# Two transformer blocks on one core: the last block's down projection with tokens on partitions, its two last RMS scales as columns, and the output sent tile by tile

## The chip, the cores and the metric

The kernel runs on one NeuronCore of a Trainium2 chip. TensorE multiplies, VectorE (DVE), ScalarE (ACT) and GpSimd (POOL) work on tiles in SBUF and PSUM, SyncE (SP) only issues DMAs here. The metric is the device time of one execution in microseconds, as the median of several runs.

## What is computed

`x` is 512 tokens by 1024 features. It goes through two layers of a first block, a final RMS norm, and one layer of a second block. Only the end of the second block is touched:

```python
h = rmsnorm_2(x, norm_mlp_pre[l])
f = jnp.square(jax.nn.relu(h @ w_ff_in[l])) @ w_ff_out[l]      # 1024 -> 4096 -> 1024
x = x + rmsnorm_2(f, norm_mlp_post[l])                         # the output
```

## The kernel before, in words

Everything is float32, and nearly every product is three TensorE instructions in fp32r: each operand is split into a rounded part (`_hi`) and the rest (`_lo`), and `triple` (L345 to L347) adds hi·hi, hi·lo and lo·hi into one PSUM bank. A matmul has a stationary operand (128x128, loaded into the array) and a moving one (128 rows of 512 columns, streamed through). The profile names the moving operand first: `psG<-hid_hi,w_hi` streams `hid_hi` past weights from `w_hi`, `psG<-w_hi,h_hi` streams weights past activations.

Activations are kept as `xT`, with features on partitions and the 512 tokens along the free axis. `pe_feature`, `pe_part` and `pe_branch` stream activations and give features on partitions; `pe_token` streams weights and gives tokens on partitions.

Weights come in units of 1 MB. For each, SP issues two 512 KB DMAs into `raw` (`w_src`, L332), ACT rounds `raw` to `w_hi` (`split_hi`, L338) and POOL subtracts to `w_lo` (L2490). There are two buffers of each, so unit k+2 is split once TensorE is through with unit k: `split_next(act, k)` stands in ACT's program where that wait is to be made. TensorE spends 48 matmuls on a unit. `tick` counts its half units, `psum_free` gives back the two pairs of `psG` banks.

Buffers are laid out by hand: first `xT`, `h_hi`, `h_lo`, `raw`, `w_hi`, `w_lo`, then small tiles (`ident`, `ones`, ..., `par` with the norm gains as columns, ...), then an "arena" of 107 KB in which every stage puts its own tiles (`at(name, kb, ...)`, at whole or half kilobytes from its start). `h_hi` begins at byte 32896 of a partition, a multiple of 64, and so do `h_lo`, `raw`, `w_hi` and `w_lo`. The arena begins at byte 119200, which is 32 past a multiple of 64, and so every tile in it begins 32 past one.

The last MLP is done in two halves of 2048 hidden features: 8 units of `w_ff_in` (each in a `Fori` loop), whose result, relu'd and squared, is split into `hid2_hi` and `hid2_lo` at the arena's start, then 8 units of `w_ff_out`. A down unit is 8 blocks of hidden features by 256 output features. The hidden tiles are the moving operand, so `psG` holds output features on partitions, two banks at a time. DVE scales each bank by the squared inverse RMS of the pre norm (a row of 512 tokens repeated on all partitions, `rms`), keeps half 0 in `y2` and adds half 1.

What follows the last matmul (all after the half-1 loop in `second_pe`, `second_act`, `second_dve`): the squares of `y2` are folded together, summed over partitions with a matmul of ones (`sum_pe`, L448), ACT takes the root (L453), DVE the reciprocal of 128x512 (L457), `post_dve` scales and adds to `xT` (L2467, L2471), TensorE transposes `xT` back in 32 pieces (L2061), DVE copies to `x_out` (L2460), and four DMAs of 512 KB send it out (L1847).

Of the kernel before, what the change touches and what calls it, by code (L numbers as in the profile page):

```python
# [23 lines left out]
ds = bass.ds  # L24
# [84 lines left out]
def build_in(nc, io, ctx):  # L109
# [137 lines left out]
    y2 = at("y2", 64, [P, KD, S])  # L247
    r2 = at("r2", 80, [P, 2, S])
    hq2 = at("hq2", 84, [P, 2, S])
    x_out = at("x_out", 0, [P, TB, D])  # L250
# [584 lines left out]
    def setup_sync(sp):  # L835
        sp.dma_start(x_tok[:, :, :], io["x"].rearrange("a (t p) d -> p (a t) d", p=P)).then_inc(ld_x.sem, 16)
        rows = [(R_ATTN, io["attn_norm"].rearrange("l (k p) -> (l k) p", p=P)),
                (R_FFN, io["ffn_norm"].rearrange("l (k p) -> (l k) p", p=P)),
                (R_DA, io["da_norm"].rearrange("l (k p) -> (l k) p", p=P)),
                (R_HG, io["hg_norm"].rearrange("l (k p) -> (l k) p", p=P)),  # L840
                (R_LB, io["hg_lb_logits"].rearrange("d l (k p) -> (d l k) p", p=P)),
                (R_FINAL, io["final_norm"].rearrange("(k p) -> k p", p=P)),
                (R_PRE2, io["norm_mix_pre_2"].rearrange("l (k p) -> (l k) p", p=P)),
                (R_POST2, io["norm_mix_post_2"].rearrange("l (k p) -> (l k) p", p=P)),
                (R_MPRE2, io["norm_mlp_pre_2"].rearrange("l (k p) -> (l k) p", p=P)),
                (R_MPOST2, io["norm_mlp_post_2"].rearrange("l (k p) -> (l k) p", p=P))]
# [1037 lines left out]
    def second_pe(pe):  # L1884
# [149 lines left out]
        for half, vf, kf, vd, kd in ((0, V_FA, K_FA, V_DA, K_DA), (1, V_FB, K_FB, V_DB, K_DB)):  # L2034
            with pe.Fori(0, 4) as i:
                for s in range(2):
                    jm, b = step(JB + kf // 2, kf % 2, s)
                    pe_feature(pe, i + (UB + vf // 2), s, i + jm, b, h_hi, h_lo,
                               mlp_tile if half == 0 and s == 0 else None)
            if half == 0:  # L2040
                sum_pe(pe, DEPTH, 3, sq_x2)
            for c in range(4):
                jm, b = jn(kd + c)
                bank_ready(pe, jm, b)
                for v in range(2):
                    m, s = un(vd + 2 * c + v)

                    def hidden_tile(k, v=v, half=half):
                        pe.wait_ge(f2_lod.sem, HT2 * half + KD * v + k + 1)

                    pe_part(pe, m, s, b, hid2_hi, hid2_lo, KD * v, KD, v == 0, v == 1,
                            hidden_tile if c == 0 else None)
        sum_pe(pe, DEPTH, 4, sq)

        for h in range(2):
            for k in range(4):
                pe.wait_ge(x2_ok.sem, KD + 4 * h + k + 1)
                for t in range(TB):
                    if h and k == 0:
                        pe.wait_ge(o_cp.sem, t + 1)  # L2060
                    mm = pe.transpose(psH[:, t, k * P:(k + 1) * P], xT[:, 4 * h + k, t * P:(t + 1) * P],  # L2061
                                      ident[:, :])
                    if k == 3:
                        mm.then_inc(o_tr.sem, 1)
# [53 lines left out]
    def second_act(act):  # L2118
# [103 lines left out]
        for half, vf, kf in ((0, V_FA, K_FA), (1, V_FB, K_FB)):  # L2222
            with act.Fori(0, 4) as i:
                for s in range(2):
# [9 lines left out]
                    for j in range(2):  # L2234
# [4 lines left out]
            if half == 0:  # L2239
                rms_act(act, DEPTH, 3)  # L2240
            for k in range(8):
                if half and k % 2 == 0 and k:
                    act.wait_ge(y_ok.sem, k // 2 + 4)
                    square_pair(act, DEPTH, 3, k // 2 - 1, y2, sq)
                split_next(act, (V_DA, V_DB)[half] + k)
        act.wait_ge(y_ok.sem, 8)
        square_pair(act, DEPTH, 3, 3, y2, sq)
        rms_act(act, DEPTH, 4)
# [38 lines left out]
    def second_dve(dve):  # L2287
# [136 lines left out]
        for half, vf, kf, vd, kd in ((0, V_FA, K_FA, V_DA, K_DA), (1, V_FB, K_FB, V_DB, K_DB)):  # L2424
# [17 lines left out]
            for c in range(4):
                b = jn(kd + c)[1]
                if half and c >= 2:
                    fold(dve, DEPTH, 3, c - 1, sq)
                for j in range(2):
                    dve.wait_ge(tick.sem, Tn(vd + 2 * c + 1, j))
                    y = y2[:, 2 * c + j, :] if half == 0 else xtmp[:, j, :]
                    mm = tt(y, psG[:, 2 * b + j, :], rms[:, :], ALU.mult)
                mm.then_inc(psum_free[b].sem, 1)  # L2450
                if half:
                    dve.drain()
                    tt(y2[:, 2 * c:2 * c + 2, :], y2[:, 2 * c:2 * c + 2, :], xtmp[:, :, :], ALU.add)\
                        .then_inc(y_ok.sem, 1)
                    dve.drain()
        fold(dve, DEPTH, 3, 3, sq)
        post_dve(dve, 4, R_MPOST2)
        for n in range(8):
            dve.wait_ge(o_tr.sem, n + 1)
            dve.tensor_copy(x_out[:, n % TB, (n // TB) * S:(n // TB + 1) * S], psH[:, n % 4, :]).then_inc(o_cp.sem, 1)  # L2460
# [86 lines left out]
```

## Time and profile before

| | |
|---|---|
| median of 3 runs | 2508.78 us (2506.7 to 2508.93) |
| the profiled execution | 2509.79 us, its span 2507.60 us |
| TensorE busy | 2397.1 us, 96% of the span |
| DVE, ACT, POOL busy | 1298.4, 814.1, 862.1 us |
| mean granted TensorE clock | 0.978 |
| last matmul of the last product starts | 2471.32 us |

The span runs from the first to the last instruction of the execution; the device time is some 2 us more. Busy times overlap, so they do not add up to the span.

### The profile page before, as it was taken

What the parts mean: (1) busy time and instruction counts of PE and PEld (TensorE: products, weight loads), DVE (VectorE), ACT (ScalarE), POOL (GpSimd) and SP (SyncE); (2) the same over time, 40 slices, a digit from 0 to 9 for tenths busy, and PEclk for the clock granted to TensorE, in tenths of its full rate; (3) what the DMA queues carried; (4) which work ended last, traced back from release to release, by engine and by line L of the source; (5) the groups of instructions that cost most, each with busy time, mean ns of one, the idle gap of its engine ahead of it and who ended that gap; (6) DMA issues with size and microseconds to landing.
All of it is one profiled execution on the core that took longest, in us unless ns stands there. A gap on an engine that the chain in (4) does not pass through costs nothing.

```text
span 2507.6 us, 28122 instructions
## 1 busy us (share of the span) xinstructions
PE 2397.1 (96%) x11057; PEld 1911.8 (76%) x11057; DVE 1298.4 (52%) x1593; ACT 814.1 (32%) x909; POOL 862.1 (34%) x198
## 2 busy tenths in 40 slices
PE   6998999999998999989999999999999996999996
PEld 5888776788886888886667888887887774888884
DVE  6476344454446554664435534486457546631624
ACT  4232334332222332323343322222326523322320
POOL 2322122344443343222224444444323222443440
PEclk9999999999999999999999999999999997999997
DMA  5332133344445443322223444454844232444440
GB/s 123 85 77 58 34 68 68 84 91 93 100 100 118 126 99 87 68 51 47 62 61 85 100 100 94 90 139 114 172 101 82 63 74 52 96 89 101 94 91 34
DMA packets 200167, 217.50 MB, mean 87 GB/s; under 512 B 14456, under 2 KB 181512, under 8 KB 199304
## 3 DMA queue, kind: packets, MB, share of 16 engines
q1 hardware_dynamic: 200072, 216.16, 39.8%
q8 instruction: 69, 1.13, 0.2%
q14 instruction: 26, 0.21, 0.0%
HBM read 206.40 MB, written 9.73 MB: 86 GB/s over the span
## 4 chain that ended last, share of the span: by engine, by line
issue 57%; PE 26%; POOL 13%; DVE 3%; DVEq 1%; ACT 1%; POOLq 0%; ACTq 0%
POOL w_lo L2490 12%; PE psG L345 8%; PE psG L346 8%; PE psG L347 8%; PE psH L2004 1%; PE psH L1989 1%; DVE xT L2471 0%; DVEq L2469 0%; PE psH L2017 0%; PE psH L1957 0%; DVE rms L457 0%; DVE y L2467 0%; PE psH L448 0%; DVE sq L422 0%; POOLq L2487 0%
## 5 line engine op out<-in xcount | busy, mean ns | idle before, releaser
L2490 POOL TENSOR_TENSOR w_lo<-raw,w_hi 128x2048 fp32r<-128x2048 f32 x186 | 860.5, 4627 | 1592.9 <-ACT w_hi L338 1592.9
L345 PE MATMUL psG<-h_hi,w_hi 128*128 128x512 f32 x1640 | 653.8, 399 | 16.4 <-DVE h_lo L466 12.3
L338 ACT CAST w_hi<-raw 128x2048 fp32r<-128x2048 f32 x186 | 354.7, 1907 | 921.5 <-PE psG L347 907.1
L347 PE MATMUL psG<-h_hi,w_lo 128*128 128x512 f32 x1640 | 644.0, 393 | 0.0
L346 PE MATMUL psG<-h_lo,w_hi 128*128 128x512 f32 x1640 | 643.8, 393 | 0.0
L345 PEld LDWEIGHTS psG<-h_hi,w_hi 128*128 128x128 f32 x1640 | 310.6, 189 | 120.9 <-issue 45.3
L347 PEld LDWEIGHTS psG<-h_hi,w_lo 128*128 128x128 f32 x1640 | 310.9, 190 | 66.3
L346 PEld LDWEIGHTS psG<-h_lo,w_hi 128*128 128x128 f32 x1640 | 311.1, 190 | 63.7 <-issue 1.4
L345 PE MATMUL psG<-hid_hi,w_hi 128*128 128x512 f32 x608 | 242.6, 399 | 6.1 <-POOL w_lo L2490 6.1
L346 PE MATMUL psG<-hid_lo,w_hi 128*128 128x512 f32 x608 | 241.0, 396 | 0.0
L347 PE MATMUL psG<-hid_hi,w_lo 128*128 128x512 f32 x608 | 240.9, 396 | 0.0
L345 PEld LDWEIGHTS psG<-hid_hi,w_hi 128*128 128x128 f32 x608 | 114.5, 188 | 34.9 <-POOL w_lo L2490 6.6
L346 PEld LDWEIGHTS psG<-hid_lo,w_hi 128*128 128x128 f32 x608 | 114.6, 188 | 28.1 <-issue 0.5
L347 PEld LDWEIGHTS psG<-hid_hi,w_lo 128*128 128x128 f32 x608 | 114.5, 188 | 28.1
L1308 DVE TENSOR_TENSOR hid_lo<-ht,hid_hi 128x512 f32 x44 | 113.7, 2622 | 41.8 <-ACT hid_hi L1159 41.8
L345 PE MATMUL psG<-w_hi,h_hi 128*128 128x512 f32 (+1 forms) x320 | 123.3, 385 | 0.0
L2431 DVE TENSOR_TENSOR hq<-r 128x512 f32<-128x512 f32 x32 | 84.9, 2692 | 72.0 <-ACT r L2232 72.0
L347 PE MATMUL psG<-w_hi,h_lo 128*128 128x512 f32 (+1 forms) x320 | 121.3, 379 | 0.0
L346 PE MATMUL psG<-w_lo,h_hi 128*128 128x512 f32 (+1 forms) x320 | 121.2, 379 | 0.0
L775 DVE TENSOR_REDUCE stat<-psH 128x1 f32<-128x512 f32 x64 | 41.2, 686 | 141.6 <-PE psH L720 141.6
L1303 DVE TENSOR_TENSOR ht<-ht,psG 128x512 f32<-128x512 f32 x44 | 30.2, 687 | 130.3 <-PE psG L347 130.0
L345 PE MATMUL psG<-m_hi,w_hi 128*128 128x512 f32 x192 | 76.2, 397 | 1.6 <-DVE m_lo L1276 0.8
(417 smaller groups left out, 3012.8 us busy)
## 6 DMA issues: line engine op xcount, KB each, us to landing
raw<-in_w_in_dram SPq DMA_DIRECT2D x122, 512.0 KB, 6.4
raw<-in_w_gate_dram SPq DMA_DIRECT2D x44, 512.0 KB, 5.9
raw<-in_w_up_dram SPq DMA_DIRECT2D x44, 512.0 KB, 6.3
raw<-in_w_down_dram SPq DMA_DIRECT2D x32, 512.0 KB, 6.3
raw<-in_w_ff_in_dram SPq DMA_DIRECT2D x32, 512.0 KB, 6.2
raw<-in_w_ff_out_dram SPq DMA_DIRECT2D x32, 512.0 KB, 6.2
raw<-in_w_o_dram SPq DMA_DIRECT2D x16, 512.0 KB, 5.6
raw<-in_w_down_dram SPq DMA_DIRECT2D x16, 384.0 KB, 5.4
```

The costliest lines, as they stand in the source:

```text
L338: act.copy(w_hi[:, s, :], raw[:, s, :]).then_inc(hi_done.sem, 1)
L345: pe.matmul(out, a_hi, b_hi, start=first, stop=False)
L346: pe.matmul(out, a_hi, b_lo, start=False, stop=False)
L347: return pe.matmul(out, a_lo, b_hi, start=False, stop=last)
L775: dve.tensor_reduce(stat[:, it % 2, c:c + 1], psH[:, c, :], AX.X, ALU.max, negate=True).then_inc(sc_max.sem, 1)
L1303: mm = dve.tensor_tensor(ht[:, j, :], ht[:, j, :], psG[:, 2 + j, :], ALU.mult)\
L1308: dve.tensor_tensor(hid_lo[:, ds(i * 2 + j, 1), :].rearrange("p a t -> p (a t)"), ht[:, j, :], hid_hi[:, ds(i * 2 + j, 1), :].bitcast(F32) ...
L1989: mm = pe.matmul(psH[:, j // 2, (j % 2) * 256:(j % 2) * 256 + w], q2[rows, j, blk_n * P:(blk_n + 1) * P], k2[rows, k0:k0 + w], start=True, ...
L2004: mm = pe.matmul(psH[HD * g:HD * g + HD, 2, :], v2[:, kb, HD * g:HD * g + HD], pT[:, i, :], start=i == 0, stop=i == len(parts) - 1)
L2431: tt(hq2[:, j, :], r2[:, j, :], r2[:, j, :], ALU.mult).then_inc(f2_q.sem, 1)
L2490: pool.tensor_tensor(w_lo[:, s, :], raw[:, s, :], w_hi[:, s, :].bitcast(F32), ALU.subtract)\
```

## The change

The down units of the last MLP are cut another way: 4 blocks of hidden features by all 512 columns of one half of the output (`v % 4` picks the hidden features, `v // 4` the output half). The hidden tiles become the stationary operand and the weights the moving one, as in `pe_token`, so all four `psG` banks hold one token tile of 128 tokens each, and four units add into them. Each down unit is still 48 matmuls of 512 columns.

With tokens on partitions a scale per token is one number per partition. The sum of squares of the pre norm becomes four matmuls with two columns each instead of one with 512; its inverse `r3c` is 128x4. ACT takes half 0 from PSUM (`down_first`), DVE adds half 1 (`down_second`). The residual `xT` is transposed during half 0, after units 3 and 6, and ACT copies it to `x2t`. The last unit ends token tile by token tile: DVE adds, ACT squares with an accumulated sum and takes the root, POOL multiplies by the gain (`gain_row`, a new broadcast DMA of 128x1024), DVE inverts one column and does two fused multiply-adds, and SP sends each half tile (8 DMAs of 256 KB).

The last gain is no longer a column of `par`: one DMA of the setup goes (`par_rows` from `norm_mlp_post_2`), and `par` has 96 columns instead of 104. With that the arena begins 32 bytes lower, at byte 119168, a multiple of 64. `h_hi` to `w_lo` stay where they were.

```diff
-R_ATTN, R_FFN, R_DA, R_HG, R_LB, R_FINAL, R_PRE2, R_POST2, R_MPRE2, R_MPOST2, R_ALL = (
-    0, 16, 32, 40, 48, 64, 72, 80, 88, 96, 104)
+R_ATTN, R_FFN, R_DA, R_HG, R_LB, R_FINAL, R_PRE2, R_POST2, R_MPRE2, R_ALL = (
+    0, 16, 32, 40, 48, 64, 72, 80, 88, 96)
...
-                (R_MPOST2, io["norm_mlp_post_2"].rearrange("l (k p) -> (l k) p", p=P))]
...
-        pe.wait_ge(ld_par.sem, 160)
+        pe.wait_ge(ld_par.sem, 144)
...
+            for v in range(8):
+                r0, c = (half * HT2 + 4 * (v % 4)) * P, S * (v // 4)
+                w_src(*un(vd + v), io["w_ff_out_2"][0, r0:r0 + 4 * P, c:c + S].rearrange("(k p) c -> p k c", p=P), sp)
+                if half and v == 3:
+                    sp.wait_ge(tick.sem, Tn(V_FB + 7, 1))
+                    sp.dma_start(gain_row[:, :], io["norm_mlp_post_2"].rearrange("l d -> (l d)").partition_broadcast(P))\
+                      .then_inc(ld_gain.sem, 16)
...
+            for h in range(2):
+                sp.wait_ge(o_ok.sem, 2 * t + h + 1)
+                sp.dma_start(out[:, t, S * h:S * h + S], x2t[:, t, S * h:S * h + S]).then_inc(st_out.sem, 16)
...
+            for v in range(8):
+                pe_down(pe, half, v, vd, kd)
+                if half == 0 and v in (3, 6):
+                    pe.wait_ge(r3_ok.sem, 1)
+                    pe.wait_ge(x2_ok.sem, KD)
+                    if v == 6:
+                        pe.wait_ge(x2_cp.sem, 2)
+                    for t in range(2):
+                        c = slice((t + 2 * (v // 6)) * P, (t + 2 * (v // 6) + 1) * P)
+                        for k in range(KD):
+                            mm = pe.transpose(psH[:, 2 * t + k // 4, (k % 4) * P:(k % 4 + 1) * P], xT[:, k, c],
+                                              ident[:, :])
+                        mm.then_inc(x2_tr.sem, 1)
...
+    def pe_down(pe, half, v, vd, kd):
...
+        for t in range(TB):
...
             for k in range(4):
...
+                mm = triple(pe, psG[:, 2 * b + t % 2, :], hid2_hi[:, n, c], hid2_lo[:, n, c], wh[:, k, :], wl[:, k, :],
+                            n == 0, n == HT2 - 1)
+            if t % 2:
+                mm.then_inc(tick.sem, 1)
+            elif half and v == 7:
+                mm.then_inc(last_mm.sem, 1)
...
+            for v in range(8):
+                if half == 0 and v % 4 == 3:
+                    down_first(act, v // 4)
+                split_next(act, (V_DA, V_DB)[half] + v)
...
+        for t in range(TB):
+            act.wait_ge(y_ok.sem, 8 + t + 1)
+            act.activation(junk[:, t, :], y2t[:, t, S:D], ACT.Square, accum_out=ssq[:, 1, t:t + 1])
+            act.drain()
+            act.activation(r4c[:, t:t + 1], ssq[:, 1, t:t + 1], ACT.Sqrt, scale=1.0 / D, bias=ss0[:, t:t + 1])\
+               .then_inc(s_sd.sem, 1)
...
+    def down_first(act, c):
+
+        act.wait_ge(r3_ok.sem, 1)
+        for t in range(TB):
+            b = jn(K_DA + 2 * c + t // 2)[1]
+            act.wait_ge(tick.sem, Tn(V_DA + 4 * c + 3, t // 2))
+            mm = act.activation(y2t[:, t, S * c:S * c + S], psG[:, 2 * b + t % 2, :], ACT.Copy, scale=r3c[:, t:t + 1])
+            if t % 2:
+                mm.then_inc(psum_free[b].sem, 1)
+        act.drain().then_inc(y_dn.sem, 1)
...
+        for t in range(TB + 1):
+            if t < TB:
+                down_second(dve, 1, t)
+            if t:
+                dve.wait_ge(s_sd.sem, t)
+                dve.reciprocal(r4c[:, t - 1:t], r4c[:, t - 1:t])
+                dve.drain()
+                dve.wait_ge(yg_ok.sem, t)
+                for h in (slice(0, S), slice(S, D)):
+                    dve.scalar_tensor_tensor(out=x2t[:, t - 1, h], in0=yg[:, t - 1, h], scalar=r4c[:, t - 1:t],
+                                             in1=x2t[:, t - 1, h], op0=ALU.mult, op1=ALU.add).then_inc(o_ok.sem, 1)
+
+    def down_second(dve, c, t):
...
+        dve.scalar_tensor_tensor(out=y2t[:, t, S * c:S * c + S], in0=psG[:, 2 * b + t % 2, :], scalar=r3c[:, t:t + 1],
+                                 in1=y2t[:, t, S * c:S * c + S], op0=ALU.mult, op1=ALU.add).then_inc(y_ok.sem, 1)
...
+        pool.wait_ge(ld_gain.sem, 16)
+        for t in range(TB):
+            pool.wait_ge(y_ok.sem, 8 + t + 1)
+            pool.tensor_tensor(yg[:, t, S:D], y2t[:, t, S:D], gain_row[:, S:D], ALU.mult).then_inc(yg_ok.sem, 1)
```

How the order on the engines moves. DVE before, from its last product to the start of the scaling of `y`:

```order
L2449 TENSOR_TENSOR xtmp<-psG,rms 128x512 x2
L2453 TENSOR_TENSOR y_132<-y_132,xtmp 128x1024
L422 TENSOR_TENSOR sq<-sq 128x1024
L427 TENSOR_TENSOR sq<-sq 128x512
L457 RECIPROCAL rms<-rms 128x512
L2467 SCALAR_TENSOR_TENSOR y_132<-y_132,par,rms 128x512 x2
L2471 TENSOR_TENSOR xT<-xT,y_132 128x512
```

DVE now, from the second output half to the end of its program (L2526 takes a token tile out of PSUM, L2516 makes half a tile of output):

```order
L2505 TENSOR_SCALAR ss_140<-ssq,small 128x4
L2526 SCALAR_TENSOR_TENSOR y2t<-psG,r3c,y2t 128x512 x2
L2512 RECIPROCAL r4c<-r4c 128x1
L2516 SCALAR_TENSOR_TENSOR x2t<-yg,r4c,x2t 128x512 x2
L2526 SCALAR_TENSOR_TENSOR y2t<-psG,r3c,y2t 128x512
L2512 RECIPROCAL r4c<-r4c 128x1
L2516 SCALAR_TENSOR_TENSOR x2t<-yg,r4c,x2t 128x512 x2
L2526 SCALAR_TENSOR_TENSOR y2t<-psG,r3c,y2t 128x512
L2512 RECIPROCAL r4c<-r4c 128x1
L2516 SCALAR_TENSOR_TENSOR x2t<-yg,r4c,x2t 128x512 x2
L2512 RECIPROCAL r4c<-r4c 128x1
```

Each tile is finished one step behind the next tile's L2526, and one more L2516 pair ends the program.

ACT before, across the down products of half 0, where it has only weights to split:

```order
L2223 REGISTER_ALU
L2223 COMPARE_AND_BRANCH
L453 ACTIVATE rms<-psH,small 128x512
L338 CAST w_hi<-raw 128x2048 x8
L2223 UNCONDITIONAL_BRANCH
```

ACT now, in the same place:

```order
L346 CAST w_hi<-raw 128x2048 x3
L2298 ACTIVATE y2t<-psG,r3c 128x512 x4
L346 CAST w_hi<-raw 128x2048
L2276 COPY x2t<-psH 128x1024 x2
L346 CAST w_hi<-raw 128x2048 x3
L2276 COPY x2t<-psH 128x1024 x2
L2298 ACTIVATE y2t<-psG,r3c 128x512 x4
L346 CAST w_hi<-raw 128x2048
```

The four copies of each `down_first` now stand ahead of a split, and the two of the residual behind one.

TensorE now, after the fourth down unit (v = 3) in half 0, where before only triples stood (the 32 transposes were its last row):

```order
L354 MATMUL psG<-w_lo,hid_hi 128x512
L355 MATMUL psG<-w_hi,hid_lo 128x512
L2069 MATMUL psH<-ident,xT 128x128 x16
L353 MATMUL psG<-w_hi,hid_hi 128x512
L354 MATMUL psG<-w_lo,hid_hi 128x512
```

`hid` and `w` have changed places against the triples before, and 16 transposes stand between two triples; the other 16 follow unit 6.

## Rows read from the trace of the kernel before

**Rows 1.** The page: span and instructions.

```profile
span 2507.6 us, 28122 instructions
```

**Rows 2.** Timeline from the last matmul (start, us, engine, line, work, idle before).

```profile
2471.32 0.40 PE L347 MATMUL psG<-hid_hi,w_lo 128*128 128x512 f32 x1
2471.75 0.69 DVE L2449 TENSOR_TENSOR xtmp<-psG,rms 128x512 f32<-128x512 f32 x1 [4.91 <-PE psG L347]
...
2499.95 2.48 DVE L2460 COPY x_out<-psH 128x512 f32<-128x512 f32 x4 [2.49 <-PE psH L2061]
2500.67 2.89 SPq L1847 DMA_DIRECT2D out_dram<-x_out  x4
```

**Rows 3.** Stretches at full clock: busy time and count by engine, clock, DMA.

```profile
440.00:470.00 30.00, 30.00 (x131) 24.08 (x130) 12.36 (x20) 8.08 (x7) 10.39 (x3) 1.00 0.33 70
2220.00:2280.00 60.00, 60.00 (x259) 48.21 (x258) 4.15 (x6) 9.55 (x5) 26.35 (x6) 1.00 0.41 88
2320.00:2380.00 60.00, 60.00 (x267) 49.67 (x266) 38.29 (x24) 21.77 (x27) 26.47 (x6) 1.00 0.42 89
```

**Rows 4.** Timeline, TensorE: starts of hi·hi matmuls, two streams.

```profile
183.99 0.39 PE L345 MATMUL psG<-w_hi,h_hi 128*128 128x512 f32 x1
190.79 0.39 PE L345 MATMUL psG<-w_hi,h_hi 128*128 128x512 f32 x1
...
2461.05 0.40 PE L345 MATMUL psG<-hid_hi,w_hi 128*128 128x512 f32 x1
2470.85 0.40 PE L345 MATMUL psG<-hid_hi,w_hi 128*128 128x512 f32 x1
```

**Rows 5.** Groups by form, whole span: busy, mean ns; of each triple its L345.

```profile
L345 PE MATMUL psG<-hid_hi,w_hi 128*128 128x512 f32 x608 | 242.6, 399 | 6.1 <-POOL w_lo L2490 6.1
L345 PE MATMUL psG<-m_hi,w_hi 128*128 128x512 f32 x192 | 76.2, 397 | 1.6 <-DVE m_lo L1276 0.8 <-DVE m_lo L2409 0.7
L345 PE MATMUL psG<-o_hi,w_hi 128*128 128x512 f32 x160 | 63.8, 399 | 0.0
```

**Rows 6.** Waits of TensorE, whole span: total us, times, longest.

```profile
PE psH L1487 <- DVEq L1642: 11.1, 1, 11.1
PE psG L345 <- POOL w_lo L2490: 9.4, 2, 6.1
```

**Rows 7.** Timeline: one unit's split, and DVE beside POOL.

```profile
2283.93 1.91 ACT L338 CAST w_hi<-raw 128x2048 fp32r<-128x2048 f32 x1 [9.01 <-PE psG L347]
2285.92 4.61 POOL L2490 TENSOR_TENSOR w_lo<-raw,w_hi 128x2048 fp32r<-128x2048 f32 x1 [6.32 <-ACT w_hi L338]
2289.48 0.69 DVE L2449 TENSOR_TENSOR y<-psG,rms 128x512 f32<-128x512 f32 x1 [16.11 <-PE psG L347]
...
2428.99 4.61 POOL L2490 TENSOR_TENSOR w_lo<-raw,w_hi 128x2048 fp32r<-128x2048 f32 x1 [6.59 <-ACT w_hi L338]
2430.09 4.60 DVE L422 TENSOR_TENSOR sq<-sq 128x1024 f32<-128x1024 f32 x1 [1.13 <-ACT sq L417]
```

**Rows 8.** Groups by form: durations of the operations that the change adds.

```profile
L2467 DVE SCALAR_TENSOR_TENSOR y<-y,par,rms 128x512 f32<-128x512 f32 x16 | 11.9, 747 | 0.3
L2383 DVE RECIPROCAL st<-st 128x4 f32<-128x4 f32 x8 | 1.4, 178 | 0.6
L1093 ACT ACTIVATE b_v<-psG,r_col 128x512 f32<-128x512 f32 x4 | 2.6, 709 | 0.0
L751 ACT ACTIVATION_READ_ACCUMULATOR prob<-psH,stat 128x1 f32 x64 | 12.5, 195 | 0.0
```

**Rows 9.** Timeline and group: transposes at full clock, and those of the end.

```profile
1930.91 1.03 PE L2017 MATMUL psH<-ident,lg 128*128 128x128 f32 x8
L2061 PE MATMUL psH<-ident,xT 128*128 128x128 f32 x32 | 8.9, 433 | 12.7 <-DVE xT L2471 7.5 <-DVE x_out L2460 4.8
```

**Rows 10.** Setup timeline, and SP's last wait.

```profile
4.73 0.31 SPq L848 DMA_DIRECT2D par_rows<-in_norm_mlp_post_dram  x1
...
SPq L105 <- DMA out_dram<-x_out: 3.6, 1, 3.6
```

More of the change, by code:

```diff
@@ L249, in build_in @@
     hq2 = at("hq2", 84, [P, 2, S])
-    x_out = at("x_out", 0, [P, TB, D])
+    y2t = at("y2t", 64, [P, TB, D])
+    junk = at("junk", 80, [P, TB, S])
+    x2t = at("x2t", 88, [P, TB, D])
+    r3c = at("r3c", 104, [P, TB])
+    ssq = at("ssq", 104.25, [P, 2, TB])
+    ss0 = at("ss0", 104.5, [P, TB])
+    r4c = at("r4c", 104.75, [P, TB])
+    gain_row = nc.alloc_sbuf_tensor_at("gain_row", [P, D], F32, offset=h_hi_at)
+    yg = nc.alloc_sbuf_tensor_at("yg", [P, TB, D], F32, offset=h_lo_at)
     t5_dram = nc.dram_tensor("t5_dram", (QH, 3 * P), F32, kind="Internal").ap()
@@ L2053, in second_pe @@
-        sum_pe(pe, DEPTH, 4, sq)
-        for h in range(2):
-            for k in range(4):
[L2057 to L2064, printed above, removed]
+                pe.wait_ge(d_fold.sem, d_fold.at(DEPTH, 4))
@@ new lines, in second_pe @@
+                for c in range(TB):
+                    mm = pe.matmul(psH[:, 0, 2 * c:2 * c + 2], sq_x2[:, 0, c * P:(c + 1) * P], ones[:, 0:2],
+                                   start=True, stop=True)
+                mm.then_inc(d_ss.sem, 1)
+            for v in range(8):
[11 more added lines that the diff above has]
+                        mm.then_inc(x2_tr.sem, 1)
@@ new lines, in pe_down @@
+    def pe_down(pe, half, v, vd, kd):
+        m, s = un(vd + v)
+        unit_ready(pe, m, s)
+        wh = w_hi[:, s, :].rearrange("p (k c) -> p k c", k=4)
+        wl = w_lo[:, s, :].rearrange("p (k c) -> p k c", k=4)
+        for t in range(TB):
+            jm, b = jn(kd + 2 * (v // 4) + t // 2)
+            if v % 4 == 0 and t % 2 == 0:
+                bank_ready(pe, jm, b)
+            for k in range(4):
+                n = 4 * (v % 4) + k
+                if v < 4 and t == 0:
+                    pe.wait_ge(f2_lod.sem, HT2 * half + n + 1)
+                c = slice(t * P, (t + 1) * P)
+                mm = triple(pe, psG[:, 2 * b + t % 2, :], hid2_hi[:, n, c], hid2_lo[:, n, c], wh[:, k, :], wl[:, k, :],
[4 more added lines that the diff above has]
+                mm.then_inc(last_mm.sem, 1)
@@ L2238, in second_act @@
                            .then_inc(f2_hid.sem, 1)
[L2239 to L2248, printed above, removed]
+            for v in range(8):
+                if half == 0 and v % 4 == 3:
+                    down_first(act, v // 4)
+                split_next(act, (V_DA, V_DB)[half] + v)
+                if half == 0 and v in (3, 6):
+                    for t in range(2):
+                        at_t = t + 2 * (v // 6)
+                        act.wait_ge(x2_tr.sem, at_t + 1)
+                        act.copy(x2t[:, at_t, :], psH[:, 2 * t:2 * t + 2, :].rearrange("p a c -> p (a c)"))\
+                           .then_inc(x2_cp.sem, 1)
+                if half and v == 3:
+                    for t in range(TB):
+                        act.wait_ge(y_ok.sem, 4 + t + 1)
+                        act.activation(junk[:, t, :], y2t[:, t, 0:S], ACT.Square, accum_out=ssq[:, 0, t:t + 1])\
+                           .then_inc(s_sq.sem, 1)
+                    act.drain()
+        act.wait_ge(s_sq.sem, TB + 1)
+        for t in range(TB):
+            act.wait_ge(y_ok.sem, 8 + t + 1)
+            act.activation(junk[:, t, :], y2t[:, t, S:D], ACT.Square, accum_out=ssq[:, 1, t:t + 1])
+            act.drain()
+            act.activation(r4c[:, t:t + 1], ssq[:, 1, t:t + 1], ACT.Sqrt, scale=1.0 / D, bias=ss0[:, t:t + 1])\
[9 more added lines that the diff above has]
+        act.drain().then_inc(y_dn.sem, 1)
     def lg_w(n):
@@ L2438, in second_dve @@
             if half == 0:
-                inverse_rms(dve, DEPTH, 3)
-                tt(rms[:, :], rms[:, :], rms[:, :], ALU.mult)
+                dve.wait_ge(d_ss.sem, d_ss.at(DEPTH, 4))
+                dve.tensor_scalar(r3c[:, :], psH[:, 0, 0:2 * TB].rearrange("p (t two) -> p t two", two=2)[:, :, 0],
+                                  1.0 / D, eps_ap, ALU.mult, ALU.add)
                 dve.drain()
[L2442 to L2460, printed above, removed]
+                dve.reciprocal(r3c[:, :], r3c[:, :]).then_inc(r3_ok.sem, 1)
+        dve.wait_ge(y_dn.sem, 2)
+        for t in range(TB):
+            down_second(dve, 0, t)
+        dve.drain()
+        dve.wait_ge(ld_gain.sem, 16)
+        for t in range(TB):
+            tt(yg[:, t, 0:S], y2t[:, t, 0:S], gain_row[:, 0:S], ALU.mult)
@@ new lines, in down_second @@
+    def down_second(dve, c, t):
+        b = jn(K_DB + 2 * c + t // 2)[1]
+        if c and t % 2 == 0:
+            dve.wait_ge(last_mm.sem, t // 2 + 1)
+        else:
+            dve.wait_ge(tick.sem, Tn(V_DB + 4 * c + 3, t // 2))
+        dve.scalar_tensor_tensor(out=y2t[:, t, S * c:S * c + S], in0=psG[:, 2 * b + t % 2, :], scalar=r3c[:, t:t + 1],
+                                 in1=y2t[:, t, S * c:S * c + S], op0=ALU.mult, op1=ALU.add).then_inc(y_ok.sem, 1)
+        if t % 2:
+            dve.drain().then_inc(psum_free[b].sem, 1)
@@ L2491, in _ @@
                     .then_inc(lo_done.sem, 1)
+        pool.wait_ge(ld_gain.sem, 16)
+        for t in range(TB):
+            pool.wait_ge(y_ok.sem, 8 + t + 1)
+            pool.tensor_tensor(yg[:, t, S:D], y2t[:, t, S:D], gain_row[:, S:D], ALU.mult).then_inc(yg_ok.sem, 1)
     @block.scalar
```

29 lines of the change are left out of this document (10 added, 19 removed).

## The prediction

> **What bounds the kernel now.** I read the page first: the span is 2507.6 us [rows 1], and the device time of that execution, 2509.79, is 2.2 us more. The median of the runs shown, 2508.78, lies 1.0 below it. I work in differences and take them from the median.
>
> Then the timeline of the end. The last matmul starts at 2471.32 and takes 0.40, and DVE starts on its bank at 2471.75 [rows 2]. I call E = 2471.72 its end. Everything behind it, 2507.6 - 2471.7 = **35.9 us**, is one chain in which no two engines work long together: squares, fold, sum, root, a reciprocal of a full tile, sixteen DVE passes, 32 transposes, eight copies, DMA. The last copies run from 2499.95 for 2.48 us [rows 2], to 2502.43, so the last DMA and the closing of the program cost 2507.6 - 2502.43 = 5.2 us, 3.6 of them SP's wait for landing [rows 10].
>
> Before E, the stretches say that TensorE bounds the last MLP: in 60 us windows it is busy for 60.00 at full clock [rows 3]. The reader should also see two speeds in them. The down units (2220 to 2280) fit 259 matmuls into 60 us, the `w_ff_in` units (2320 to 2380) fit 267, at the same clock and the same shape. The timeline gives it exactly: with `hid_hi` streaming, 42 matmuls take 2470.85 - 2461.05 = 9.80 us, **0.2333 us** each; with `w_hi` streaming, 30 take 190.79 - 183.99 = 6.80, **0.2267** each [rows 4]. The first layer's branch products, which stream `o_hi`, have the slow speed too: 131 in 30 us [rows 3], where 0.2267 would give 132 to 134 and 0.2333 gives 129 to 131. What the slow streams share is the arena: `hid`, `o`, `m` lie there, 32 bytes past a multiple of 64; `w` and `h` lie on one. The difference, 0.0067 us, is 16 columns at 2.4 GHz, and 16 floats are 64 bytes: as if a stream of 2048 bytes that begins off such a boundary costs one piece more. That is my reading of an address listing and these rows, not something that a row names.
>
> **The sum, part by part.**
>
> *Setup.* One DMA issue of 0.31 us goes from SP's queue [rows 10], ahead of the first weights. I take -0.3 (0 to -0.3).
>
> *The arena moved by 32 bytes.* Nothing in the diff's kernel code speaks of it, but every arena tile now starts on a multiple of 64. Streams that remain there: `hid` 608 triples less the 256 of the last block's down units (16 units of 16 triples), `m` 192, `o` 160 less 32 that in the second block lie in `h_hi`'s place [rows 5]: 352 + 192 + 128 = 672 triples, 2016 matmuls. At 0.0067 each 13.4 us. Some stand ahead of a wait that ends on another engine's clock: the 11.1 us for DVE's tables and the 6.1 us for `w_lo` [rows 6] both fall in a layer's down products, with by my count of the timeline some 400 of these matmuls ahead of them, 2.7 us. So **-10.7** (0 if my reading is wrong, -13.4 if no wait eats any).
>
> *The down units.* 768 matmuls now stream `w` instead of `hid`: 768 x 0.0067 = **-5.1** (0 to -5.1; the form is that of the token units, which ran at 0.2267 [rows 4]). Their stationary tile comes from the arena now. Loads took 48.21 us for 258, 0.187 each [rows 3], hidden under 0.2267.
>
> *The scale of the pre norm.* One 512-column sum becomes four with two columns; both under a microsecond, and the full-tile reciprocal that goes had the first down product as cover. 0.
>
> *The transposes.* 32 of them enter TensorE's full stream. At full clock eight took 1.03 us [rows 9], about 0.12 each: 32 x 0.12 = **+3.9**. The same work at the end shows 433 ns each with its waits [rows 9]; nothing waits in the new place (residual and `r3c` are ready long before, `psH` is idle), but by starts there it was 0.28, which bounds this at +9.
>
> *ACT between the splits.* A split is ACT 1.91 us and POOL 4.61 [rows 7], 6.6 with latencies, and a unit is 10.9 us of matmuls: 4.3 us of slack. `down_first` stands ahead of a split twice; two of its four copies can only start when the unit has ended, 2 x 0.71 [rows 8] and a drain, 1.6 us. Queued behind them is the split, behind that POOL's, behind that TensorE two units on: ready 8.2 us after the unit's end, wanted at 10.9. 0, with 2.7 us to spare; without that cover at most 1.6 twice. The banks: the first pair is freed in the middle of the fourth unit, the second 1.6 us behind its end and wanted 5.4 behind it. 0. The gain row adds one 512 KB DMA to SP's queue, ahead of the loads of one unit that is wanted two units later. Its cover is those 22 us of matmuls; 0, and a few us once if it were gone.
>
> *The new end.* Each token tile's last 12 matmuls take 2.7 us, so tiles 0 to 3 end at E-8.2, E-5.4, E-2.7, E. DVE needs for each: L2526, 0.75; a small reciprocal, 0.18 and a drain; two L2516, 2 x 0.75 [rows 8] and gaps: 2.6 us. That alone would just keep up. But POOL multiplies by the gain as soon as L2526 is done, two SBUF inputs of 512 columns, a quarter of 4.61: 1.15 us. The rows show what such an instruction does to DVE: L422 was ready at 2430.09 and ran 4.60 us where it needs 1.2, to 1.1 us behind POOL's end at 2433.60; L2449, which reads one input from PSUM, ran its 0.69 untouched inside POOL's window [rows 7]. L2526 reads PSUM and goes through; L2516 has two SBUF inputs and waits. So a step is 0.75 + 1.25 + 1.6 = 3.6 us, longer than TensorE's 2.7. Followed through: tile 1's L2526 starts at E-5.4, its step's pair (tile 0) ends at E-1.8; tile 2's step ends at E+1.7; tile 3's L2526 E+1.8 to E+2.5, POOL to E+3.8, pair of tile 2 to E+5.4, then tile 3's small reciprocal (ACT's square, its 0.195 read-out [rows 8] and its root are done by then) and pair: **E+7.2**. If POOL never holds DVE up: E+4.5.
> The Trainium skill (SBUF — State Buffer, "SBUF: two separate sides") says that DVE and GpSimd share a port pair as an exclusive lock, held for the whole instruction. The trace agrees by L422's 4.60 us; by the rule the end is E+7.2, without it E+4.5.
> From the last L2516 to the end: before 5.2, with 2 MB in the queue within 2 us. Now the last piece is 256 KB and the seven before it are spread over 9 us. It can hardly cost more than 5.2; a floor from the 3.6 of SP's wait, less some transfer time, is 3. I take 4.1. New end: 7.2 + 4.1 = 11.3 (7.5 to 12.4) against 35.9: **-24.6**.
>
> Sum: -0.3 - 10.7 - 5.1 + 3.9 - 24.6 = **-36.8 us**, 2508.8 - 36.8 = **2472.0 us**.
>
> **Rivals.**
>
> *The arena's place doesn't matter.* Then the slow speed comes from something else that `hid`, `m`, `o` share (how high they lie, for one), and stays. For it: every slow stream lies in one region, so no row parts place from alignment. Against: the exact 16 columns. Without the 10.7: **2482.7**.
> The Trainium skill (SBUF — State Buffer, "Specifications (TRN2)") gives 16-byte lines, with a penalty for each crossing into a new one. Both arena starts are multiples of 16, so by that page moving it by 32 bytes changes nothing, and the time is this rival's; no row here shows such a line.
>
> *The slow speed belongs to the stage, not the moving tile.* Then the down units don't gain either: 2482.7 + 5.1 = **2487.8**. Against: the token units' 0.2267.
>
> *The loads of `hid` show.* 768 stationary tiles now come out of the arena. If a load took longer than a stream, each would add the excess, and the change is slower than before from (36.8 + 5.0 for 0.2%) / 768 = 0.054 us, a pitch of 0.281. A load that is not hidden at all, 0.187, would cost 144 us: **2616**. Against: the token units load activations under the same stream at 0.2267, and transposes load arena tiles within 0.12.
>
> *The end is held longer.* If the eight output DMAs queue behind one another, or each costs its landing in turn, the end is some 10 us longer: **2482**. Against: four of 512 KB ended 5.2 us behind their last.
>
> **How the numbers follow.** Forecast 0.72 (own range 2464 to 2478). Arena unchanged 0.15, no gain on streams 0.04, long end 0.04, still faster than 2464 (waits in the layers shrinking, clock) 0.03, loads or a late split that turn it slower 0.02. The range takes the low bounds, 2.7 less for waits and 3.8 for the end (2465.5), to 2464, and reaches up over the second case: **2464 to 2485**. A change under 0.2%, 5 us, can't be told from none here. Faster needs only the end's 24.6: 0.96; same 0.01; slower 0.03.
>
> **What would show it.** In the changed profile: down units with 267 matmuls in 60 us; `o` and `m` streams with 134 in 30 us instead of 131 (the arena), 2.7 us between the last unit's tiles; 32 transposes at about 0.12 in two groups; no wait of TensorE for POOL in the down stage; L2516 stretched beside POOL; last matmul some 12 us earlier than 2471.3, and some 11 us from there to the end. The prediction is wrong if arena streams still take 0.2333, if a load of `hid` takes over 0.22, or if DVE and the output take more than 15 us behind E.

## The result, and the profile after

The changed kernel takes **2469.84 us** (median of 4, 2467.76 to 2470.11) against 2508.86 (4 runs): ratio 0.9843, 95% interval 0.9826 to 0.9860, 39 us less. The forecast was 2472.0. The profiled execution took 2470.11, with a span 39.3 us shorter [rows 1]. The page's head, after:

```profile
span 2468.3 us, 28041 instructions
PE 2372.0 (96%) x11061; PEld 1909.6 (77%) x11061; DVE 1273.5 (52%) x1569; ACT 824.0 (33%) x935; POOL 866.2 (35%) x202
```

The stretches of the changed kernel (stretch, its length, busy time and count of PE, PEld, DVE, ACT, POOL, then clock, DMA share, GB/s):

```profile
440.00:470.00 30.00, 30.00 (x134) 24.86 (x133) 14.31 (x21) 7.59 (x7) 12.80 (x3) 1.00 0.33 70
860.00:890.00 30.00, 30.00 (x134) 24.85 (x133) 13.98 (x11) 10.49 (x10) 13.87 (x3) 1.00 0.47 119
2310.00:2370.00 60.00, 60.00 (x266) 49.67 (x266) 38.33 (x23) 21.78 (x28) 27.14 (x6) 1.00 0.41 88
2380.00:2440.00 60.00, 60.00 (x267) 49.67 (x266) 11.74 (x12) 15.08 (x16) 23.12 (x5) 1.00 0.45 97
```

The first answers to the `o` stretch of [rows 3], 134 matmuls instead of 131. The second lies in a layer's down products, the third in the `w_ff_in` units of half 1, the last in the down units of half 1, 267 instead of 259. The `o`, `m` and `hid` streams, and `w` past `hid`, now have the speed that only `h` and `w` had.

The timeline of its end, TensorE's last row first, then DVE, POOL, ACT and SP:

```profile
2459.43 0.39 PE L355 MATMUL psG<-w_hi,hid_lo 128*128 128x512 f32 x1
...
2457.68 0.74 DVE L2526 SCALAR_TENSOR_TENSOR y2t<-psG,r3c,y2t 128x512 f32<-128x512 f32 x1
2458.50 1.30 POOL L2564 TENSOR_TENSOR yg<-y2t,gain_row 128x512 f32<-128x512 f32 x1 [1.95 <-DVE y2t L2526]
2458.57 2.44 DVE L2516 SCALAR_TENSOR_TENSOR x2t<-yg,r4c,x2t 128x512 f32<-128x512 f32 x2
2460.93 0.74 DVE L2526 SCALAR_TENSOR_TENSOR y2t<-psG,r3c,y2t 128x512 f32<-128x512 f32 x1
2461.74 1.27 POOL L2564 TENSOR_TENSOR yg<-y2t,gain_row 128x512 f32<-128x512 f32 x1 [1.95 <-DVE y2t L2526]
2462.04 2.18 DVE L2516 SCALAR_TENSOR_TENSOR x2t<-yg,r4c,x2t 128x512 f32<-128x512 f32 x2
2464.37 1.41 DVE L2516 SCALAR_TENSOR_TENSOR x2t<-yg,r4c,x2t 128x512 f32<-128x512 f32 x2
...
2457.12 9.02 SPq L1860 DMA_DIRECT2D out_dram<-x2t  x8
```

SP's last wait in it:

```profile
SPq L105 <- DMA out_dram<-x2t: 1.7, 1, 1.7
```

TensorE ends at 2459.82 (E), 11.9 us earlier than in [rows 2]. DVE ends at 2465.78, E+6.0, and the program at 2468.3, E+8.5, where it was E+35.9. Each L2516 pair that has a POOL instruction beside it takes 2.2 to 2.4 us; the last, with POOL done, 1.41. So of the 39.3 us between the two spans 11.9 came ahead of the last matmul's end and 27.4 behind it.

### The profile page after: what moved, and what is told of

Its sections match the earlier page's. It is cut to its first block, busy times and chain, and to the rows that moved or that the text cites. A ratio compares the mean times of both kernels' runs of the same rounds, so it can differ in the third digit from the quotient of the medians.

```text
span 2468.3 us, 28041 instructions
## 1 busy us (share of the span) xinstructions
PE 2372.0 (96%) x11061; PEld 1909.6 (77%) x11061; DVE 1273.5 (52%) x1569; ACT 824.0 (33%) x935; POOL 866.2 (35%) x202
## 4 chain that ended last, share of the span: by engine, by line
issue 58%; PE 26%; POOL 13%; DVE 3%; DVEq 1%; ACT 0%; POOLq 0%; ACTq 0%
POOL w_lo L2559 13%; PE psG L353 8%; PE psG L354 8%; PE psG L355 8%; PE psH L2017 1%; PE psH L2002 1%; PE psH L2030 0%; PE psH L1970 0%; DVE x2t L2516 0%; POOLq L2556 0%; DVE xT L2540 0%; DVE y L2536 0%; DVE sq L430 0%; DVEq L2538 0%; DVE sq_y L430 0%
## 5 line engine op out<-in xcount | busy, mean ns | idle before, releaser
L353 PE MATMUL psG<-hid_hi,w_hi 128*128 128x512 f32 x352 | 138.8, 394 | 6.2 <-POOL w_lo L2559 6.2
L354 PE MATMUL psG<-hid_lo,w_hi 128*128 128x512 f32 x352 | 137.7, 391 | 0.0
L355 PE MATMUL psG<-hid_hi,w_lo 128*128 128x512 f32 x352 | 137.5, 391 | 0.0
L353 PE MATMUL psG<-w_hi,hid_hi 128*128 128x512 f32 x256 | 99.9, 390 | 0.0
L355 PE MATMUL psG<-w_hi,hid_lo 128*128 128x512 f32 x256 | 99.6, 389 | 0.0
L354 PE MATMUL psG<-w_lo,hid_hi 128*128 128x512 f32 x256 | 99.6, 389 | 0.0
L353 PEld LDWEIGHTS psG<-hid_hi,w_hi 128*128 128x128 f32 x352 | 66.5, 189 | 21.2 <-POOL w_lo L2559 7.0
```

Source lines behind the costliest of these rows:

```text
L353: pe.matmul(out, a_hi, b_hi, start=first, stop=False)
L354: pe.matmul(out, a_hi, b_lo, start=False, stop=False)
L355: return pe.matmul(out, a_lo, b_hi, start=False, stop=last)
```

## The experiments

The two kernels differ in several things at once. The runs below take apart the speed of the streams, which carried 15.8 us of the forecast on an inference, and then the end. A median of the kernel before that stands beside a run is from the same session. The changed kernel's 2469.84 is from the session of the result, and between sessions the kernel before moved by up to 1.6 us (2508.86 to 2510.42). For a stretch to compare I use the count of matmuls at full clock, as in [rows 3].

**1. Only the arena moved by 32 bytes** (kernel before):

```diff
+    sb("pad", [P, 8])
     ARENA = 107 * KB
```

> The kernel before with 32 unused bytes ahead of the arena and nothing else: the arena starts at byte 119232, a multiple of 64. If a stream pays for starting off a multiple of 64, all arena streams (o, m, hid, z; the last block's down units too) go from 0.2333 to 0.2267 us a matmul: 2928 matmuls x 0.0067 = 19.5 us at most, of which some 3 are lost ahead of waits: about 2492.5 us, with 267 matmuls in 60 us of the down units. If the slow speed comes from how high the arena lies or from the stage, it stays at 2508.9 and 259.

2500.78 us (6 runs) against 2509.73: ratio 0.9968 (0.9955 to 0.9980). The stretch of the `o` stream and one of the down units:

```profile
440.00:470.00 30.00, 30.00 (x133) 24.60 (x131) 13.38 (x21) 8.08 (x7) 11.41 (x3) 1.00 0.33 70
2210.00:2270.00 60.00, 60.00 (x264) 49.24 (x263) 5.78 (x8) 11.46 (x6) 25.73 (x6) 1.00 0.43 92
```

Neither theory: 264 in 60 us lies between 259 and 267. A third speed, 0.229 us a matmul, at a start that is a multiple of 64. The place does matter, but not as "on or off a multiple of 64".

**2. The changed kernel with its arena put back** (`sb("pad", [P, 8])` at the same place, arena at byte 119200):

> The changed kernel with 32 unused bytes ahead of the arena: it starts at 119200 again, 32 past a multiple of 64. By the alignment theory o, m, hid and z stream at 0.2333 again and the time rises by what that gave until the last MLP, about 10.8 us, to 2480.5; the last down units stream w and keep 0.2267, and their stationary tiles off the multiple cost nothing. If the place or the stage decides, 2469.8. If misaligned stationary tiles cost too, the down units show a pitch above 0.2267.

2485.76 us (4 runs): 15.9 more than the changed kernel, not 10.8. The down units (`w` streams, `hid` is stationary) did not keep 0.2267:

```profile
2380.00:2440.00 60.00, 60.00 (x260) 48.46 (x259) 21.17 (x16) 15.42 (x19) 25.71 (x6) 1.00 0.45 97
```

That is 260 in 60 us, where the changed kernel has 267; by starts in the timeline 0.2333 us each. So which operand is streamed gives nothing, and a pair with one operand in a badly placed arena is slow either way round. The forecast's 5.1 us had the wrong reason.

**3. Everything moved by 32 bytes** (kernel before):

```diff
+    sb("pad", [P, 8])
     xT = sb("xT", [P, KD, S])
```

> The kernel before with 32 unused bytes ahead of the very first tile: h, raw and w now start 32 past a multiple of 64, the arena on one. By the alignment theory the speeds change places: streams of h and w at 0.2333, of o, m and hid at 0.2267. 1928 triples x 3 x 0.0067 = +38.7 against -19.5, less what waits absorb of both: about 2525 us. By the place theory nothing changes places, 2508.9.

2509.91 us (10 runs) against 2509.73: ratio 1.0001 (0.9991 to 1.0010). Nothing changed places. Stretches of `o` (slow), of `h` (fast, though it now starts 32 past a multiple of 64) and of the down units:

```profile
440.00:470.00 30.00, 30.00 (x130) 24.09 (x129) 12.57 (x20) 8.08 (x7) 10.57 (x3) 1.00 0.36 70
600.00:630.00 30.00, 30.00 (x134) 24.86 (x133) 10.93 (x12) 6.24 (x8) 13.06 (x3) 1.00 0.45 90
2220.00:2280.00 60.00, 60.00 (x259) 48.19 (x258) 4.15 (x6) 9.62 (x6) 26.60 (x6) 1.00 0.44 88
```

The arena starts at byte 119232 here, the very byte of experiment 1, and is slow where it was faster there. The alignment theory falls. What is the same in this kernel and in the kernel before is how far each operand lies from the other. That became the new theory: the distance between the stationary and the moving operand decides, at first with a period of 128 bytes.

**4. The distance 96 past a multiple of 128** (changed kernel, pad of 24 words ahead of the arena):

> The changed kernel with 96 unused bytes ahead of the arena. New theory, from the three runs before: what counts is how far the two operands lie apart, modulo 128 bytes: 0 gives 0.2267 us a matmul, 64 gives 0.2293, 32 gives 0.2333, whichever of the two is streamed and wherever the pair lies. 96 is as far from 128 as 32: 0.2333 expected in o, m, hid and the last down units, 2485.8 us like the run with 32. If instead a step of its own belongs to each distance, some other value between 0.2267 and 0.2333.

2485.60 us (4 runs), as expected. `o`: 130 matmuls in 30 us.

**5. w moved away from h, the arena with it** (changed kernel):

```diff
+    sb("pad", [P, 8])
     w_hi = sb("w_hi", [P, 2, UNIT], F32R)
```

> The changed kernel with 32 unused bytes between raw and w_hi: w_hi and w_lo start 32 bytes later, the arena too (byte 119200, 32 past a multiple of 64), h_hi and h_lo stay. By the theory of the distance all pairs of h and w become slow (1928 triples, 0.2267 to 0.2333) and the pairs of w with the arena stay fast at an arena start that was slow before: +38.7 us at most, about 2505, with 259 instead of 267 matmuls in 60 us of the w_ff_in units. By a theory of absolute places w's own streams and the arena's would be slow and h's fast: about 2490.

2506.57 us (10 runs), 36.7 more than the changed kernel. The stretches of `o`, of `h`, and of the `w_ff_in` units of half 1:

```profile
440.00:470.00 30.00, 30.00 (x134) 24.86 (x133) 12.18 (x20) 5.49 (x5) 9.24 (x2) 1.00 0.43 94
600.00:630.00 30.00, 30.00 (x130) 24.16 (x129) 11.95 (x13) 8.86 (x9) 11.11 (x3) 1.00 0.50 105
2330.00:2390.00 60.00, 60.00 (x259) 48.33 (x258) 33.81 (x21) 23.43 (x28) 24.24 (x6) 1.00 0.49 104
```

Now the speeds did change places: the arena pairs are fast at byte 119200, the slow start of the kernel before, and every pair of `h` and `w` is slow, with `h` where it always was. Distance, not address.

**6. The distance 128 past a multiple of 256** (kernel before, pad of 24 words):

> The kernel before with 96 unused bytes ahead of the arena (byte 119296): 0 modulo 128 away from w, as in the changed kernel, and no other edit. All arena pairs at 0.2267: the 10.7 us to the last MLP and 5.1 in its down units, 15.8 less: 2493. That the down units gain 5.1 without streaming w would show that the change of roles gives nothing. If streaming w gives the down units their gain, they stay at 0.2333 and the time is 2498.

2510.13 us (10 runs) against 2510.42, ratio 0.9996 (0.9987 to 1.0006): no change, and my period of 128 was wrong. `o` and the down units:

```profile
440.00:470.00 30.00, 30.00 (x131) 24.33 (x130) 11.77 (x19) 8.09 (x7) 9.76 (x3) 1.00 0.33 70
2220.00:2280.00 60.00, 60.00 (x259) 48.27 (x258) 4.15 (x6) 9.54 (x5) 26.80 (x6) 1.00 0.41 88
```

Counting again, the fast distances so far were 37120 and 49152, both multiples of 256; 37248 is 128 past one.

**7. The distance a multiple of 256, nothing else** (kernel before, pad of 56 words):

> The kernel before with 224 unused bytes ahead of the arena (byte 119424, 37376 from w_hi, a multiple of 256; in the changed kernel it is 37120, a multiple too, and in the run with 96 bytes it was 37248, 128 past one). If the period is 256, all arena pairs take 0.2267 without any other edit: 10.7 to the last MLP and 5.1 in its down units less, 2493; the down units show 267 matmuls in 60 us though they stream hid. If only the changed kernel's own distance or its form is fast, 2509.

2493.88 us (4 runs) against 2509.37: ratio 0.9939 (0.9922 to 0.9956), 15.5 less, expected 15.8. `o` and the down units of half 0, which stream `hid` as before:

```profile
440.00:470.00 30.00, 30.00 (x134) 24.85 (x133) 13.89 (x21) 8.10 (x7) 11.80 (x3) 1.00 0.33 70
2220.00:2280.00 60.00, 60.00 (x267) 49.69 (x266) 3.46 (x5) 9.55 (x5) 25.42 (x6) 1.00 0.42 93
```

This is the share of 39 us that has nothing to do with tokens on partitions: 15.5 us came from 32 bytes of `par`. The rest of the change is worth 24.0, from 2493.88 to 2469.84: the 27.4 behind the last matmul, less 3.5 for the transposes.

**8 and 9. The other distances** (changed kernel, pads ahead of `w_hi` and of the arena: 160 and 192 bytes, then 224 and 256).

> The changed kernel with 160 unused bytes ahead of w_hi and 192 ahead of the arena: w is 160 (modulo 256) from h, and the arena 192 from w. If only multiples of 256 are fast, both kinds are slow: h with w at 0.2333 (an odd multiple of 32), the arena with w at 0.2293 (an odd multiple of 64, as 64 gave) or 0.2333; about 2515. If the period were 128 for some pairs, 192 would equal 64 exactly.

> The changed kernel with 224 unused bytes ahead of w_hi and 256 ahead of the arena: w is 224 (modulo 256) from h, the arena 0 modulo 512 from w, where it is 256 modulo 512 in the changed kernel. h with w at 0.2333; the arena with w at 0.2267 if 256 is the period, and faster than that if 512 is one too; about 2505.

2519.84 and 2507.54 us, one run each. `o` and `h` of the first, then of the second:

```profile
440.00:470.00 30.00, 30.00 (x130) 24.20 (x129) 11.57 (x19) 5.93 (x6) 9.23 (x2) 1.00 0.41 92
600.00:630.00 30.00, 30.00 (x131) 24.11 (x130) 13.12 (x12) 7.34 (x7) 10.79 (x3) 1.00 0.50 103
```

```profile
440.00:470.00 30.00, 30.00 (x134) 24.83 (x133) 12.20 (x21) 6.33 (x7) 9.20 (x2) 1.00 0.41 93
600.00:630.00 30.00, 30.00 (x130) 24.13 (x129) 12.16 (x13) 8.85 (x9) 10.30 (x4) 1.00 0.50 105
```

The arena at 37376, a multiple of 512, is no faster than at 37120. All together, by distance in bytes; the third and fourth columns are with the arena tile or `h` streamed, the last with `w` streamed and the other one stationary:

| distance, modulo 256 | pair | matmuls in 30 us | us each | us each, `w` streamed |
|---|---|---|---|---|
| 49152, 37120, 37376: 0 | h-w, arena-w | 134 | 0.2267 | 0.2267 |
| 37152, 49184: 32 | arena-w, h-w | 131, 130 | 0.2333 | 0.2333 |
| 37184: 64 | arena-w | 133 | 0.229 | not run |
| 37216: 96 | arena-w | 130 | 0.233 | 0.234 |
| 37248: 128 | arena-w | 131 | 0.232 to 0.233 | not run |
| 49312: 160 | h-w | 131 | 0.233 | 0.234 |
| 37312: 192 | arena-w | 130 | 0.233 | 0.233, then 0.229 |
| 49376: 224 | h-w | 130 | 0.233 | 0.233 |

The last two columns are from starts in the timelines. All tiles here start at multiples of 32 bytes, so finer distances were not tried.

64 and 192 differ, and so do the two directions of one pair. The down units of experiment 8, which stream `w` past `hid` at 192, show both speeds: the first row is from the first four units of half 0, the second from half 1.

```profile
2240.00:2270.00 30.00, 30.00 (x130) 24.29 (x129) 6.92 (x6) 6.89 (x7) 13.85 (x3) 1.00 0.37 76
2425.00:2485.00 60.00, 60.00 (x264) 49.24 (x263) 15.68 (x13) 13.20 (x15) 26.63 (x6) 1.00 0.45 97
```

The second is the 264 of experiment 1, and one reading covers both: count the distance from the stationary tile to the moving one, with its sign. The moving tile is 64 past the stationary one when an arena tile 64 past `w` is streamed, and also when `w` is streamed past an arena tile that lies 192 past it. In the same way `w` past `hid` in experiment 4 and `w` past `h` in experiment 8 are both 160, and both take 0.234. I made this reading from the rows afterwards and no run was built to test it. The four units at 0.233 speak against it: they run so up to the transposes behind unit 3, and the twelve units behind those take 0.229 at the same distance. Why is open, and nothing shows what in the chip the two reads meet in.

**10. The end without POOL's multiplication** (changed kernel; the gain of the second output half is left out, L2516 reads `y2t` for it):

```diff
...
-            pool.tensor_tensor(yg[:, t, S:D], y2t[:, t, S:D], gain_row[:, S:D], ALU.mult).then_inc(yg_ok.sem, 1)
+            pool.sem_inc(yg_ok.sem, 1)
```

> The changed kernel without POOL's four multiplications of the second output half by its gain (the gain of that half is left out of the result; DVE reads y2t instead of yg). If POOL's instruction holds DVE's two-input passes back, L2516 pairs drop from 2.2 or 2.4 us to 1.5, tile 3's L2526 starts with the end of its product and the last pair ends about 4.3 us behind the last matmul instead of 6.0: 2468.2 us. If DVE is slow there for another reason, the pairs stay at 2.2 and the time at 2469.8.

2466.94 us (4 runs). TensorE's last row starts at 2457.93, E = 2458.32; tile 3 on DVE:

```profile
2458.36 0.75 DVE L2527 SCALAR_TENSOR_TENSOR y2t<-psG,r3c,y2t 128x512 f32<-128x512 f32 x1 [0.40 <-PE psG L355]
...
2461.71 0.75 DVE L2516 SCALAR_TENSOR_TENSOR x2t<-y2t,r4c,x2t 128x512 f32<-128x512 f32 x1
```

DVE takes tile 3 as soon as it is there and ends at E+4.1 (expected 4.3; 6.0 with POOL). The stretched passes were POOL's doing. The median is 2.9 us below the changed kernel's, of which 1.9 are these; the rest lies ahead of E, where this kernel is the same.

**11. The residual of two tiles left in PSUM** (changed kernel; transposes of tiles 0 and 3 first, then 1 and 2, which ACT doesn't copy):

```diff
...
+                    res = psH[:, 2 * (t - 2) + h.start // S, :] if t - 1 in (1, 2) else x2t[:, t - 1, h]
                     dve.scalar_tensor_tensor(out=x2t[:, t - 1, h], in0=yg[:, t - 1, h], scalar=r4c[:, t - 1:t],
-                                             in1=x2t[:, t - 1, h], op0=ALU.mult, op1=ALU.add).then_inc(o_ok.sem, 1)
+                                             in1=res, op0=ALU.mult, op1=ALU.add).then_inc(o_ok.sem, 1)
```

> The changed kernel, with the transposed residual of token tiles 1 and 2 left in PSUM (tiles 0 and 3 are transposed and copied first, 1 and 2 after unit 6 and not copied), so that L2516 reads one SBUF input and one from PSUM for them. If POOL's lock is what stretches the pairs, those of tiles 1 and 2 take 1.4 us beside POOL instead of 2.4 and 2.2, tile 3's L2526 starts within 0.2 us of its product, and the last pair ends some 4.5 us behind the last matmul: 2468.3. If PSUM reads are slowed too, no change, 2469.8.

2468.71 us (4 runs, 2465.99 to 2472.03). The timeline of tile 2's pair with POOL beside it, and the last pair; TensorE's last matmul ends at 2460.13:

```profile
2461.03 1.27 POOL L2565 TENSOR_TENSOR yg<-y2t,gain_row 128x512 f32<-128x512 f32 x1 [0.92 <-DVE y2t L2527]
```

```profile
2460.20 0.75 DVE L2527 SCALAR_TENSOR_TENSOR y2t<-psG,r3c,y2t 128x512 f32<-128x512 f32 x1
2461.09 0.16 DVE L2512 RECIPROCAL r4c<-r4c 128x1 f32<-128x1 f32 x1
2461.32 1.41 DVE L2517 SCALAR_TENSOR_TENSOR x2t<-yg,r4c,psH 128x512 f32<-128x512 f32 x2
...
2462.88 1.42 DVE L2517 SCALAR_TENSOR_TENSOR x2t<-yg,r4c,x2t 128x512 f32<-128x512 f32 x2
```

With one input from PSUM the pair takes 1.41 us inside POOL's window, and DVE ends at E+4.2 with the whole result computed. The 1.1 us between the medians are too few to tell from no change; the 1.8 us in the end are seen in the rows alone.

## Why the prediction was right, point by point

- **The sum.** 36.8 us forecast, 39.0 measured by the medians, 39.3 by the spans of the profiled executions. Ahead of E 12.2 forecast, 11.9 measured; behind it 24.6 forecast, 27.4 measured (both from the spans).
- **Setup, -0.3.** It measured 0. TensorE was about 1.0 us ahead at 44 us, and the first layer's attention gave it back: the first matmul of the `o` stream starts at the same time in both kernels. After, and before:

```profile
428.21 0.50 PE L353 MATMUL psG<-o_hi,w_hi 128*128 128x512 f32 x1
```

```profile
428.19 0.51 PE L345 MATMUL psG<-o_hi,w_hi 128*128 128x512 f32 x1
```

- **The arena, -10.7.** From there to the last `w_ff_in` matmul of half 0 (2204.20 before, 2193.79 after) it gave 10.4. The size was right and the reading behind it, that "a stream of 2048 bytes that begins off such a boundary costs one piece more", was wrong: experiment 3 streams from off the boundary at full speed, and 5 has the arena off it and fast. The distance to the other operand decides. The rows of before could not part the two, because there the fast pairs lie a multiple of 256 apart and start on a multiple of 64 as well. I had taken "the exact 16 columns" as evidence for a mechanism; it was none. That the size came out all the same is luck: by my reading any multiple of 64 gives the full 15.8 us of this step and the next, and the multiple of 64 in experiment 1 gave 9.0. Shrinking `par` by 32 bytes happened to leave the arena a multiple of 256 from `w`.
- **The down units, -5.1.** The size was right (half 1 took 2.6 us less), the step wrong: it is not that they stream `w` "instead of `hid`". Experiment 2 streams `w` and is slow, experiment 7 streams `hid` and is fast. This gain belongs to the arena too.
- **The rival by the Trainium skill** (SBUF — State Buffer, "Specifications (TRN2)": 16-byte lines, by which 32 bytes change nothing) gave 2482.7. Experiment 7 speaks against it: an arena moved by 224 bytes alone, also a multiple of 16, gave 15.5 us.
- **The transposes, +3.9.** 3.5 measured. Between two triples of the changed kernel:

```profile
2238.26 0.39 PE L355 MATMUL psG<-w_hi,hid_lo 128*128 128x512 f32 x1
2238.50 1.91 PE L2069 MATMUL psH<-ident,xT 128*128 128x128 f32 x16
2240.16 0.48 PE L353 MATMUL psG<-w_hi,hid_hi 128*128 128x512 f32 x1
```

  The gap of 2240.16 - 2238.26 = 1.90 us stands where 0.23 would be, the first matmul behind it has 0.08 on top: 1.75 each time, twice.
- **ACT between the splits, 0.** The timelines of ACT and POOL behind that unit:

```profile
2238.69 1.27 ACT L2298 ACTIVATE y2t<-psG,r3c 128x512 f32<-128x512 f32 x2 [4.12 <-PE psG L355]
2240.41 1.91 ACT L346 CAST w_hi<-raw 128x2048 fp32r<-128x2048 f32 x1 [0.45 <-issue]
```

```profile
2242.39 4.61 POOL L2559 TENSOR_TENSOR w_lo<-raw,w_hi 128x2048 fp32r<-128x2048 f32 x1 [7.95 <-ACT w_hi L346]
```

  The split starts 1.8 us behind the unit's end at 2238.65 (1.6 forecast). Its unit is ready at 2247.0 and wanted at 2251.1, 48 matmuls behind the 2240.16 at which the unit before it starts. TensorE waited for nothing from 2120 us on.
- **The new end, 11.3.** 8.5 measured. DVE's part, E+7.2, came to E+6.0: the hold by POOL was there as forecast (a step takes 3.25 us, longer than TensorE's 2.7), but a step was 3.6 in my sum, because a pair of L2516 takes 1.41 us and not the 1.6 that I added up with gaps. By the Trainium skill's lock (SBUF — State Buffer, "SBUF: two separate sides") a two-input pass waits for GpSimd and one that reads PSUM doesn't; experiments 10 and 11 agree, with 4.1 and 4.2 instead of 6.0. What follows DVE's end was the worst-sized term: 2.5 us against 4.1. SP's wait for landing fell from 3.6 to 1.7 us; my floor of 3 was above it. The last piece is now half the size and has fewer bytes queued ahead of it; no run separates the two.

The sum held because each size came from rows that measure the same thing, and for the 15.8 us because the arena landed well: the end gave 2.8 us more than priced, the transposes cost 0.4 less, the arena and the setup gave 0.3 less each. Of the reasons, two were wrong.

## What to carry to other kernels

Where TensorE is the bound, compare the pitch of one form of matmul across stages before anything else: 3% hid in tile placement here, and a pad of 224 bytes in the old kernel gave 15.5 us for no edit of the work. Place operands that are multiplied with each other a multiple of 256 bytes apart (shown for fp32r matmuls of 512 columns, and better than each of the seven other distances tried, in steps of 32 bytes), and when an edit changes the size of any small tile, look at where everything behind it has moved. For a chain behind the last matmul, a scale that becomes a column and an output that leaves by tile took 27.4 us off; beside a GpSimd pass, give DVE one input from PSUM.

## What the runs showed of the hardware that I had not expected

- An fp32r matmul of 512 columns at full clock takes 0.2267 us when its stationary and its moving operand lie a multiple of 256 bytes apart in a partition, whichever of the two is streamed and whatever their own addresses are. At every other multiple of 32 it is slower: 0.229 with an arena tile streamed 64 past `w`, 0.232 to 0.234 at 32, 96, 128, 160 and 224, and at 192 0.233 with the arena tile streamed, but 0.229 in most units with `w` streamed (seven distances of the arena from `w`, four of `w` from `h`).
- Loads of the stationary operand are hidden all the same (0.187 us each at either speed), so it is the start-to-start time that grows by 3%, without a wait in the profile.
- A pair of DVE passes with two SBUF inputs that started 0.07 us behind a GpSimd pass of 1.30 us took 2.44 us instead of 1.41. With one input of each in PSUM the pair took 1.41 us beside the same GpSimd pass.
